# Gated recurrence of a decoder trunk: pair products cut to 32-token diagonal blocks, log k instead of k, three level buffers

## The reference, cut to what matters

```python
log_f = jnp.logaddexp(jnp.log(lb), jnp.log1p(-lb) + jax.nn.log_sigmoid(fl))
k = (1.0 - lb) * jax.nn.sigmoid(-fl)
qa = jax.nn.silu(q)

def step(S, blk):                       # one chunk of tokens
    qc, kc, vc, lc = blk
    L = jnp.cumsum(lc, axis=2)
    inter = jnp.einsum('bhtk,bhkv->bhtv', qc * jnp.exp(L), S)
    diff = jnp.where(causal, L[:, :, :, None, :] - L[:, :, None, :, :], -jnp.inf)
    A = jnp.einsum('bhtk,bhsk,bhtsk->bhts', qc, kc, jnp.exp(diff))
    intra = jnp.einsum('bhts,bhsv->bhtv', A, vc)
    L_end = L[:, :, -1:, :]
    S = jnp.exp(L_end[:, :, 0, :, None]) * S + jnp.einsum('bhsk,bhsv->bhkv', kc * jnp.exp(L_end - L), vc)
    return S, inter + intra
```

## Time and profile before

| | us |
|---|---|
| median of three runs | 2465.13 |
| profiled execution, its own time | 2473.21 |
| its span, first to last instruction | 2471.3 |
| TensorE busy in the span | 2330.7 (94%) |
| VectorE busy | 1298.9 (53%) |
| GpSimd busy | 1087.2 (44%) |
| ScalarE busy | 487.6 (20%) |

### The profile page before, as it was taken

One profiled execution on the slowest core, in us unless ns is written; L12 is line 12 of the kernel. 1 busy time (PEld: TensorE's weight loads), 2 busy tenths in 40 slices (PEclk: granted clock), 3 DMA queues, 4 the chain that ended last, 5 costly groups with the idle time before them and its releaser, 6 DMA issues.

```text
span 2471.3 us, 33961 instructions
## 1 busy us (share of the span) xinstructions
PE 2330.7 (94%) x10472; PEld 1793.0 (73%) x10472; DVE 1298.9 (53%) x1975; ACT 487.6 (20%) x916; POOL 1087.2 (44%) x1274
## 2 busy tenths in 40 slices
PE   8998987999998999999899989879999989999997
PEld 6775776677776777777676757667777767777775
DVE  0634687533456666671216347874333666666622
ACT  1534211211113101100125332112111121010002
POOL 0000724556663666734300008254666637676342
PEclk9999986999999999999999999869999999999998
DMA  6222110222212222222032211103221222121220
GB/s 214 80 73 61 39 73 1 104 77 77 77 52 98 85 71 82 80 70 83 35 122 84 81 44 39 73 1 113 77 77 69 69 98 85 68 85 68 77 71 38
DMA packets 51600, 183.60 MB, mean 74 GB/s; under 512 B 7234, under 2 KB 27970, under 8 KB 37762
## 3 DMA queue, kind: packets, MB, share of 16 engines
q1 hardware_dynamic: 50882, 178.49, 21.2%
q10 hardware_dynamic: 576, 3.36, 0.3%
HBM read 172.64 MB, written 9.18 MB: 74 GB/s over the span
## 4 chain that ended last, share of the span: by engine, by line
PE 84%; DVE 7%; issue 4%; SPq 4%; ACT 1%; DMA 0%; POOL 0%; DVEq 0%; ACTq 0%; POOLq 0%
PE ps L1154 23%; PE ps L1082 18%; PE ps L1192 16%; PE ps L857 14%; PE ps L1398 3%; PE ps L1325 1%; PE ps L878 1%; SPq L694 1%; SPq L706 1%; PE ps L1075 1%; DVE r L2171 1%; PE ps L1067 1%; SPq L699 1%; DVE xT L1945 1%; DVE r L634 1%
## 5 line engine op out<-in xcount | busy, mean ns | idle before, releaser
L857 PE MATMUL ps<-xT,wring 128*128 128x288 f32 (+2 forms) x1152 | 282.2, 408 | 1.4 <-DVE o_mla L2112 1.4
L857 PEld LDWEIGHTS ps<-xT,wring 128*128 128x128 f32 x1152 | 219.9, 191 | 62.5 <-issue 1.7
L634 POOL TENSOR_TENSOR r<-lq 128x288 f32<-128x288 f32 (+1 forms) x40 | 28.6, 715 | 530.1 <-PE ps L1426 530.1
L1154 PE MATMUL ps<-lq,mreg 128*128 128x288 f32 x1008 | 251.3, 406 | 0.0
L1154 PEld LDWEIGHTS ps<-lq,mreg 128*128 128x128 f32 x1008 | 191.5, 190 | 52.9
L1507 ACT ACTIVATE r<-ps 128x288 f32<-128x288 f32 (+7 forms) x268 | 113.3, 428 | 562.8 <-PE ps L1082 255.4
L1154 PE MATMUL ps<-xT,wring 128*128 128x288 f32 x672 | 169.8, 406 | 0.0
L1154 PEld LDWEIGHTS ps<-xT,wring 128*128 128x128 f32 x672 | 127.7, 190 | 35.3
L1082 PE MATMUL ps<-r,kbuf 128*128 128x288 f32 x576 | 143.6, 406 | 0.0
L2585 POOL TENSOR_TENSOR kbuf<-o_mla 128x288 f32<-128x288 f32 x42 | 33.3, 792 | 225.6 <-DVE o_mla L2350 225.6
L1082 PEld LDWEIGHTS ps<-r,kbuf 128*128 128x128 f32 x576 | 109.4, 190 | 30.2
(11 more groups left out here) (377 smaller groups left out, 4747.9 us busy)
## 6 DMA issues: line engine op xcount, KB each, us to landing
wring<-w_stream SPq DMA_DIRECT2D x100, 1024.0 KB, 4.9
side<-w_stream SPq DMA_DIRECT2D x18, 704.0 KB, 4.3
r<-pages_in SPq DMA_DIRECT2D x80, 128.0 KB, 2.1
vbuf<-w_stream SPq DMA_DIRECT2D x12, 512.0 KB, 3.7
r<-w_stream SPq DMA_DIRECT2D x12, 512.0 KB, 3.6
wring<-w_stream SPq DMA_DIRECT2D x8, 704.0 KB, 4.2
r<-w_stream SPq DMA_DIRECT2D x6, 704.0 KB, 4.2
mreg<-pages_in SPq DMA_DIRECT2D x32, 128.0 KB, 2.1
```

Of the source, the lines that this page charges most:

```text
L634: eng.tensor_tensor(hi, lhi, mid, ALU.subtract)
L857: mm = pe.matmul(out[0:w.shape[-1], a * 512:a * 512 + hi - lo], w, x[:, lo:hi], start=(k == 0), stop=(k == len(pairs) - 1))
L1154: mm = pe.matmul(up_sum[name], ws[:, k * P:(k + 1) * P], xs[:, k, :], start=(k == 0), stop=(k == HK - 1))
```

## The change

In the stage of the recurrence:

1. A chunk's pairs are cut at 32 tokens. Diagonal and levels 1 to 16 are computed on the four 32-token diagonal blocks alone, as 32x32 products, 6 x 4 of them, into one PSUM bank of 192 columns; levels 64 and 32 as four products of 32 weight columns into the other bank. A sample step has 4 x 2 products of 32x32.
2. VectorE's mask and sum cover 192 columns in place of 896, the sum goes to PSUM, and a third operation spreads the sums over a 128x128 matrix of scores by a block mask. ScalarE copies the off-diagonal parts (three copies) and signals `hg_full`, for which TensorE's sums wait.
3. log k replaces k: `log_k` (VectorE, one subtraction, and one on GpSimd) goes into the lower halves' exponents, so they need no product with k. The products of the lower halves and of the decayed k go; the diagonal needs `k_now` = exp(log k + L). The four exponentials of k in the projection stage go.
4. Three level buffers, `LEV_BUF = (2, 0, 1, 2)`, so that head 2's exponents can be made before head 0 is done. GpSimd makes the differences of all levels for all heads; VectorE's differences and end products go. VectorE multiplies the upper halves of heads 2 and 3 at n = 4 and n = 13.
5. ScalarE takes the exponentials of heads 2 and 3 in steps: levels after n = 0, 1, 2 and 10, 11, 12, ends after n = 7 and 13. `value_blocks` is one operation in place of eight. TensorE's exceptions in order (`late`) go.

The diff, cut to its core:

```diff
+SUB = 32
+N_DIAG = LEVELS.index(SUB) + 1
+LEV_BUF = (2, 0, 1, 2)
+LEVEL_STEPS = {0: (2, 0, 2), 1: (2, 2, 5), 2: (2, 5, 7), 10: (3, 0, 2), 11: (3, 2, 5), 12: (3, 5, 7)}
+END_STEPS = {7: 2, 13: 3}
...
             for half, out, t0, t1 in levels(h, first, end):
                 lo, hi, _ = parts(out, half)
                 eng.tensor_tensor(hi, lhi, mid, ALU.subtract)
-                ins = eng.tensor_tensor(lo, mid, llo, ALU.subtract)
+                ins = eng.tensor_tensor(lo, alo, mid, ALU.add)
...
                 eng.tensor_tensor(hi, hi, qhi, ALU.mult)
-                ins = eng.tensor_tensor(lo, lo, klo, ALU.mult)
...
+        def ends_differences(eng, h):
+            eng.tensor_tensor(k_now[h % 2], log_k[:, h, :], logf[:, h, :], ALU.add)
+            src, k = (ap[:, h, SEQ:T].rearrange("p (n b) -> p n b", b=DEC_SEQ) for ap in (logf, log_k))
+            return eng.tensor_tensor(decayed[:, h % 2, 1, SEQ:T].rearrange("p (n b) -> p n b", b=DEC_SEQ),
+                                     src[:, :, DEC_SEQ - 1:DEC_SEQ].broadcast_to([P, DEC_BATCH, DEC_SEQ]), k, ALU.add)
...
                     pe.wait_ge(*lev_ready.at(l, h + 1))
                     if h >= 2:
-                        pe.wait_ge(*big_ready.at(l, h - 1))
+                        pe.wait_ge(*late_ready.at(l, h - 1))
                 if n >= 2:
-                    pe.wait_ge(*hg_masked.at(l, n - 1))
+                    pe.wait_ge(*hg_scores.at(l, n - 1))
...
+                for v in range(N_DIAG if c < N_CHUNK else 1 + SMALL_LEVELS):
+                    for i in range(w // SUB):
+                        lo, hi = SUB * i, SUB * (i + 1)
+                        if v == 0:
+                            k, q = k_now[h % 2][:, t0 + lo:t0 + hi], q_hg[:, h, t0 + lo:t0 + hi]
+                        else:
+                            k = q = lev[v - 1][:, at + lo:at + hi]
+                        mm = pe.matmul(diag[lo:hi, v * SUB:(v + 1) * SUB], k, q, start=True, stop=True)
                 if c < N_CHUNK:
+                    m = lev[N_DIAG]
+                    for i in range(2):
+                        pe.matmul(off[SUB * i:SUB * (i + 1), 0:64], m[:, at + SUB * i:at + SUB * (i + 1)],
+                                  m[:, at + 64:at + P], start=True, stop=True)
+                    m = lev[N_DIAG - 1]
+                    for a in range(2):
+                        lo = 64 * a
+                        mm = pe.matmul(off[lo:lo + SUB, 64:64 + SUB], m[:, at + lo:at + lo + SUB],
+                                       m[:, at + lo + SUB:at + lo + 64], start=True, stop=True)
...
             def hg_sums(l, n):
-                pe.wait_ge(*hg_scores.at(l, n + 1))
                 if c < N_CHUNK:
+                    pe.wait_ge(*full_at(l, n))
...
                 for n in range(N_HG):
-                    late = n + 1 in (2 * (N_CHUNK + 1), 3 * (N_CHUNK + 1))
...
                     if n + 1 < N_HG:
                         hg_pair_scores(l, n + 1)
+                    hg_sums(l, n)
...
                 def decays_ends(h):
                     act.wait_ge(*lev_diff.at(l, 2 * h + 2))
+                    act.activation(k_now[h % 2], k_now[h % 2], ACT.Exp)
                     act.activation(decayed[:, h % 2, 0, :], logf[:, h, :], ACT.Exp)
-                    act.activation(decayed[:, h % 2, 1, :], decayed[:, h % 2, 1, :], ACT.Exp).then_inc(lev_exp.sem, 1)
+                    for c in range(N_CHUNK):
+                        end = (c + 1) * P
+                        act.activation(decayed[:, h % 2, 1, end - P:end], log_k[:, h, end - P:end], ACT.Exp,
+                                       bias=logf[:, h, end - 1:end])
...
                     copy(k_rows[0:w, n % 2, :], bank[6][0:w, 0:P]).then_inc(hg_k_rows.sem, 1)
+                    if c < N_CHUNK:
+                        act.wait_ge(*hg_scores.at(l, n + 1))
+                        full, off = scores_hg[:, n % 2, :], bank[2 * (n % 2) + 1]
+                        copy(full[0:64, 64:P], off[0:64, 0:64])
+                        for a in (0, 64):
+                            ins = copy(full[a:a + SUB, a + SUB:a + 64], off[a:a + SUB, 64:64 + SUB])
+                        ins.then_inc(hg_full.sem, 1)
+                    if n in LEVEL_STEPS:
+                        decays_levels(*LEVEL_STEPS[n])
+                    if n in END_STEPS:
+                        decays_ends(END_STEPS[n])
...
-                    dve.tensor_tensor(masked[0:w, 0:nl, 0:w], raw[:, 0:nl, 0:w], mask8[0:w, 0:nl, 0:w],
+                    dve.tensor_tensor(masked[0:w, 0:nl, :], raw, mask[0:w, 0:nl, :], ALU.mult).then_inc(hg_masked.sem, 1)
+                    summed = bank[2 * (n % 2)][0:w, N_DIAG * SUB:(N_DIAG + 1) * SUB]
+                    dve.tensor_reduce(summed, masked[0:w, 0:nl, :].rearrange("p l t -> p t l"), AX_X, ALU.add
+                                      ).then_inc(hg_summed.sem, 1)
-                    dve.tensor_reduce(scores_hg[0:w, n % 2, 0:w],
-                                      masked[0:w, 0:nl, 0:w].rearrange("p l t -> p t l"), AX_X, ALU.add
+                    dve.tensor_tensor(scores_hg[0:w, n % 2, 0:w].rearrange("p (n t) -> p n t", t=SUB),
+                                      summed.unsqueeze(1).broadcast_to([w, w // SUB, SUB]),
+                                      own_block[0:w, 0:w // SUB, :], ALU.mult).then_inc(hg_scores.sem, 1)
...
                 for n in range(N_HG + 1):
-                        level_differences(dve, h + 1, SMALL_LEVELS, len(LEVELS)).then_inc(big_diff.sem, 1)
...
+                    if n < N_HG:
+                        pair_sums(n)
+                    if n >= 1:
                         update(n - 1)
+                    if n in (4, 13):
+                        h = 2 + n // 10
+                        dve.wait_ge(*lev_exp.at(l, h + 1))
+                        level_scaled(dve, h).then_inc(late_ready.sem, 1)
...
+                pool.wait_ge(*prep_dve.at(l, 8))
+                pool.wait_ge(*q_rope.at(l, 2))
+                pool.tensor_tensor(log_k, log_k, logf, ALU.subtract).then_inc(log_k_ready.sem, 1)
...
                 differences(l, 0)
+                ends(l, 0)
                 differences(l, 1)
+                ends(l, 1)
+                scaled(l, 0)
+                ends_scaled(l, 0)
+                value_blocks(l, 0)
+                scaled(l, 1)
+                ends_scaled(l, 1)
+                pool.wait_ge(*pool_d_ready.at(l, POOL_GROUPS))
+                differences(l, 2)
+                pool.wait_ge(*hg_upd.at(l, N_CHUNK + 2))
+                ends(l, 2)
+                value_blocks(l, 1)
+                ends_scaled(l, 2)
+                differences(l, 3)
+                pool.wait_ge(*hg_upd.at(l, 2 * (N_CHUNK + 2)))
+                ends(l, 3)
+                value_blocks(l, 2)
+                ends_scaled(l, 3)
+                pool.wait_ge(*hg_upd.at(l, 3 * (N_CHUNK + 2)))
+                value_blocks(l, 3)
```

More of the change, by code:

```diff
@@ L617, in parts, with levels @@
             return v[:, :, 0:half], v[:, :, half:2 * half], v[:, :, half - 1:half]
-        def levels(h, first=0, end=len(LEVELS)):
+        def levels(h, first, end):
+            b = LEV_BUF[h]
             for v in range(first, end):
-                half = LEVELS[v]
+                yield LEVELS[v], level[b][v], 0, SEQ
                 if v < SMALL_LEVELS:
-                    yield half, level_small[h % 2][:, v, :], T
-                else:
-                    yield half, level_big[h % 2][:, v - SMALL_LEVELS, :], SEQ
@@ L628, in level_differences @@
-        def level_differences(eng, h, first, end):
-            for half, out, n in levels(h, first, end):
+                    yield LEVELS[v], level_s[b][v], SEQ, T
+        def level_differences(eng, h, first=0, end=len(LEVELS)):
+            for half, out, t0, t1 in levels(h, first, end):
                 lo, hi, _ = parts(out, half)
-                llo, lhi, mid = parts(logf[:, h, 0:n], half)
-                mid = mid.broadcast_to([P, n // (2 * half), half])
+                _, lhi, mid = parts(logf[:, h, t0:t1], half)
+                alo, _, _ = parts(log_k[:, h, t0:t1], half)
+                mid = mid.broadcast_to([P, (t1 - t0) // (2 * half), half])
@@ L648, in ends_scaled, with level_scaled @@
-        def ends_scaled(eng, h):
-            eng.tensor_tensor(decayed[:, h % 2, 0, :], decayed[:, h % 2, 0, :], q_hg[:, h, :], ALU.mult)
-            return eng.tensor_tensor(decayed[:, h % 2, 1, :], decayed[:, h % 2, 1, :], k_hg[:, h, :], ALU.mult)
+        def level_scaled(eng, h, first=0, end=len(LEVELS)):
+            for half, out, t0, t1 in levels(h, first, end):
+                _, hi, _ = parts(out, half)
+                _, qhi, _ = parts(q_hg[:, h, t0:t1], half)
+                ins = eng.tensor_tensor(hi, hi, qhi, ALU.mult)
+            return ins
@@ L1022, in hg_pair_scores @@
-                if c < N_CHUNK:
-                    for v in range(SMALL_LEVELS, top - 1):
-                        m = big[:, v - SMALL_LEVELS, t0:t1]
```

(7 more changed lines are left out.)

210 lines of the change are left out of this document (88 added, 122 removed).

## The result

| | before | after |
|---|---|---|
| median, us | 2466.49 (2464.92 to 2468.68, four runs) | 2385.90 (2383.31 to 2387.18, four runs) |
| profiled execution, its span, us | 2471.3 | 2381.5 |

The ratio is 0.9653, interval 0.9636 to 0.967: 80.6 us faster. The forecast was 2423, with a range down to 2388; the direction was right, the gain was almost twice the one forecast. Two executions further down, one of e9 (5268 us) and one of e12 (3412 us), lie far outside the rest, and the ratios leave them out.

A forecast was written before the change was run, and what follows sets the result against it. VectorE was taken to bound the recurrence's chunks, TensorE after the change. A layer's stage summed to 77.5 us at full clock plus 20 for the clock, 97.5 against 118.0 and 118.8: 42 us less, 2423 us, range 2388 to 2470.

The forecast's parts named there:

- What bounds the kernel: Recurrence stage, 118.0 and 118.8 us: VectorE bounds the chunks at 3.22 us each; outside the stage nothing moves over 2 us.
- A chunk on VectorE and ScalarE: Recurrence chunk: VectorE 1.5 us in place of 3.2, ScalarE's copies some 0.6, pair's end to `hg_full` 1.85 us.
- allowance of 0.5 us for the first exponentials: Recurrence stage: 0.5 us a layer of new waiting for the first exponentials.
- A chunk on TensorE: Recurrence chunk: 56 records at 0.030 us, 1.9 us a pair, 2.56 with sums; TensorE bounds it, chain covered by 0.7.
- rival (d): TensorE's pairs: products on different column groups overlap, pair about 0.9 us, 11 us a layer less, 2401 us; chance 0.14.
- The value blocks: Sample steps on TensorE: value blocks 3.7 us a head, which with the wait hardly change at the 1.2 GHz clock.
- The clock: Recurrence stage: narrow moving operands and the wait lower TensorE's clock after sample steps, 5.0 us a head, 20 a layer.
- The waits: TensorE in the recurrence stage: 3.5 us at pair(15), 1.5 at pair(10), 1.3 a head for the states' updates.
- Rival (c): Helpers become the bound: head 3's differences late for ScalarE or VectorE stands beside GpSimd; up to 12 us a layer, 2447; chance 0.13.
- The removal of 17.8 us from VectorE: Recurrence stage: the big levels' differences of heads 2 and 3, 17.8 us, leave VectorE for GpSimd.
- (a): Clock stays at 1.2 GHz for nearly the whole recurrence stage: 10 us a layer slower, 2485 us; chance 0.12.
- (b): TensorE's pairs: a record costs 0.055 us whatever its width, 24 us a layer more, 2471, up to 2491; chance 0.08.

The follow-up runs named there:

- e9: The kernel with head 3's differences made early, with three early levels in place of four: 2372.3 us, ratio 0.96 to the kernel before.
- e12: The changed kernel with head 3's differences made early, run unchanged a second time: 2374.2 us, ratio 0.961 to the kernel before.
- e1: Changed kernel with the two loops of the 32x32 products swapped, so neighbours sit on the same 32 columns of the array: 2400.3 us, ratio 0.9707.
- e13: Changed kernel with each of a chunk's six diagonal products made as one dense 128x128 product in place of four 32x32: 2404.1 us, ratio 0.9735.
- e5: Changed kernel without the eight 128x8 products by which a sample step adds the samples' old states to their outputs: 2374.8 us, ratio 0.9612.
- e3: Changed kernel with head 3's four smallest levels' differences before head 2's ends, exponentials and ends sooner, upper-half products in smaller portions: 2372.2 us, ratio 0.9597.
- e4: Kernel before, with only the big levels' differences of heads 2 and 3 moved from VectorE to GpSimd: 2467.8 us, ratio 0.9985.
- e6: Changed kernel with the diagonal blocks as two 64x64 products a level in place of four 32x32: 2400.7 us, ratio 0.9719.
- e2: Changed kernel with VectorE's strided sum over the six diagonal products made three times in place of once: 2402.3 us, ratio 0.9717.

## Why the prediction was wrong

*What bounds the kernel.* Right: VectorE bounded the chunks, and nearly all of the gain lay in this stage. Outside of it 1.5 us moved.

*A chunk on VectorE and ScalarE.* Right: VectorE's durations within 0.04 us, ScalarE's three copies 0.49 us for 0.6. The path from a pair's end to `hg_full`, taken at 1.85, is right within 0.1 in the first chunk (the pair ends at about 324.9, the copies at 326.66). What the sum missed is ScalarE's other work in that path: its allowance of 0.5 us for the first exponentials came out at 2.3 (1.26, 0.18 and 0.89), the one term that was too low.

*A chunk on TensorE.* This is a step that failed: "I take 0.030, near the proportion". It was 9 ns. The 56 records of a pair went from 1.7 us to about 0.75. In e1's order the proportion nearly holds (23 ns); the rest is overlap of neighbouring column groups, rival (d), which I had put at 0.14 on the strength of the earlier trace rows. "So TensorE bounds the chunk ... covered by 0.7 us" fell with it: at full clock the chain bounds, at half clock TensorE does. Rival (d) gave 11 us a layer less; e13 against the changed kernel shows 9.7 and 9.0.

The rule of the Trainium skill ("TensorEngine Tiling (Array Packing)", Key Properties) that tiles work in parallel holds here where products alternate over quarters (9 for 23 ns); for halves (35 ns) no run shows how much. The section Instruction Overhead of that page of the Trainium skill gives a matmul about 60 cycles of overhead: by estimate 25 ns at 2.4 GHz, and 50 for a record of two passes. The 23 ns of e1 speak against two passes, and the 9 ns on alternating groups lie below either.

*The value blocks.* The second step that failed: "5 are value blocks and wait, which hardly change with it". They take 1.98 us at full clock and 3.78 at half. I had read one row, taken at half clock (the earlier trace rows has 0.56 from 349 on), as a price at full clock: (3.72 - 1.98) x 4 = 7 us a layer.

*The clock.* The third, of size only: 20 us a layer. Estimated from the profile after, TensorE is busy for some 31 us of the stage at half clock (5.83, 15.32 and 9.3 us in three stretches, and 0.8), which is some 16 us more than the same work at full clock; in e13 (busy 73 of 83.5 us at 0.83) the same reckoning gives some 13. The two together account for e13's 14.0: value blocks 7, clock 7 (e13's waits, 10.5 us, are the forecast's 10.7). In the changed kernel the stage then is work some 44 us (66.8 forecast; 15 of the difference are pairs, 7 value blocks), clock 16 (20), waits 14 (10.7): 73.8. These three are my split of one stretch, not measured apart. The prediction put the fall down to narrow operands and the wait; e5 takes the first alone out, and nothing here shows more.

*The waits.* Pair(15) 3.1 us for 3.5, behind the mechanism named; after the value blocks 1.98, 1.22, 1.21 for 1.3 each. Pair(10) did not wait for GpSimd (1.5 forecast); ScalarE's ends cost 1.4 at pair(9) in its place, and 0.8 at pair(14). Head 0's for ScalarE are told above. The level products at n = 4 were called free; that is so within about 0.7 us (the wait of 1.98 against 1.22 elsewhere), and e5 shows how thin the cover is. Rival (c), the helpers, was half true: it did not make the kernel slower than the forecast, but head 0's waits for ScalarE are its kind, and e3 gets 11 to 14 us out of the helpers' order.

*The removal of 17.8 us from VectorE.* Right in the sum, but e4 shows that it is worth 1 to 6 us for the whole kernel by itself.

*Rivals (a) and (b).* The clock stood at half for half of the stage, not for 80%; a record of 32 columns cost less than half of 0.055 even unoverlapped. Both are out.

## What to carry over

Before you price a product whose width no row shows, ask where its neighbour sits: four 32-column records on four column groups cost less than two in one place do (36 ns for 46), and the order of two loops decides it. When an engine serves a chain and does other work between, price the chain with that work in its queue: ScalarE's exponentials made one step 3.26 us where the chain alone made 1.93. Read a duration of TensorE together with the granted clock of its stretch, or a half-clock price enters a full-clock sum. When work leaves an engine, follow who can begin it when: the same move was worth 1 to 6 us without the rest of the change, and 11 to 14 more came with an order in which GpSimd's idle 6 us held the work that ScalarE was waiting for.

## What the runs showed of the hardware

- fp32 records with 128 rows, 32 weight and 32 moving columns follow each other at 9 ns if products alternate over four column groups (changed kernel) and at 23 ns on one (e1); 64 by 64 alternating over two halves at 35 ns (e6); dense ones at 112. All at the full granted clock.
- Of the eight falls of the granted clock in the two stages of the changed kernel, three came in a wait (at about 341.2, 371.9 and 1542.7) and five with TensorE busy on eight-column products or value blocks (354.9, 395.8, 1522.2, 1559.8 and 1576.8). Without the eight-column products it still fell, in the first stage of e5 four times and each time in a wait. In the changed kernel's first stage it stayed at 1.00 from 324 to 341 through waits of 0.63, 1.26, 0.18 and 0.89 us; in e2 it fell at 332.4, just after one of 1.40 that no sample step preceded. Which property of the stretch it follows was not settled.
- GpSimd's differences took 10.2 us a head, beside a VectorE busy for 0.13 us of them (308.4 to 318.6) and for 5.22 (351.5 to 361.7). On the line of the earlier trace rows the longest operation was 0.99 us in the profile after, but ahead of the stage, beside a busy GpSimd, an operation of 64 columns took 6.22 us, and with GpSimd idle 0.22, so what the earlier trace rows shows is shorter but not gone:

```profile
285.10 6.22 DVE L2177 SCALAR_TENSOR_TENSOR r<-r 128x64 f32<-128x64 f32 x1
...
308.11 0.22 DVE L2177 SCALAR_TENSOR_TENSOR r<-r 128x64 f32<-128x64 f32 x1
```
